# Changing the order in which the first two weight tiles of a projection meet the split activations, and the order inside a head norm, an attention and a scan

## The reference

```python
# one head of layer 0: o is normed per head (subln), then all heads meet wo
o = jnp.einsum('bhqk,bkhe->bqhe', a, v)
o = rmsnorm(o, subln) * (1.0 - lam_init)
y = o.reshape(...) @ wo
x = x + g1 * y
# every projection in front of an attention or feed-forward part reads a modulated norm
h = rmsnorm(x, norm_mix[i]) * (1.0 + sc1) + sh1
```

## Time and profile before

| what | value |
|---|---|
| median of 3 runs | 3529.85 us (3528.49 to 3533.06) |
| the profiled execution, its own time | 3529.11 us |
| its span (first to last instruction) | 3527.3 us |
| mean granted TensorE clock | 0.969 of 2.4 GHz |
| PE busy | 3268.6 us, 93% of the span |
| DVE, ACT, POOL busy | 2269.5, 1466.2, 332.9 us |
| head norm block, from the trace | about 444 to 477 us |
| neighbourhood attention | about 1324 to 1509 us |
| hgrn scan | about 2472 to 2611 us |

### The profile page before, as it was taken

One profiled execution on the slowest core, in us unless ns is written; L12 is line 12 of the kernel. 1 busy time (PEld: TensorE's weight loads), 2 busy tenths in 40 slices (PEclk: granted clock), 3 DMA queues, 4 the chain that ended last, 5 costly groups with the idle time before them and its releaser, 6 DMA issues. The chain is left out here.

```text
span 3527.3 us, 46837 instructions
## 1 busy us (share of the span) xinstructions
PE 3268.6 (93%) x18680; PEld 2681.7 (76%) x18680; DVE 2269.5 (64%) x2972; ACT 1466.2 (42%) x1948; POOL 332.9 (9%) x214
## 2 busy tenths in 40 slices
PE   7998989999998998889999998889889989999996
PEld 5887768888887896778787868779667766777774
DVE  6467756656656317758776555575665357888885
ACT  5216723212122116633233343433433246777774
POOL 0020000000000000000000004321100013222221
PEclk8999989999999999999999999999989999999998
DMA  6550013453542221045654229211013249999993
GB/s 238 192 172 13 1 48 93 134 167 119 168 127 87 66 75 55 22 126 184 212 176 148 55 76 273 57 37 49 25 42 90 72 185 363 383 374 369 378 364 109
DMA packets 371656, 522.46 MB, mean 148 GB/s; under 512 B 19618, under 2 KB 313122, under 8 KB 345872
## 3 DMA queue, kind: packets, MB, share of 16 engines
q1 hardware_dynamic: 362112, 503.25, 42.6%
q0 software_dynamic: 9360, 16.72, 1.4%
HBM read 484.46 MB, written 51.90 MB: 152 GB/s over the span
## 5 line engine op out<-in xcount | busy, mean ns | idle before, releaser
L270 DVE TENSOR_TENSOR lo<-exp_raw,exp_hi 128x2048 fp32r<-128x2048 f32 x192 | 438.9, 2290 | 65.3 <-ACT exp_hi L3548 65.3
L3548 ACT CAST exp_hi<-exp_raw 128x2048 fp32r<-128x2048 f32 x192 | 366.5, 1913 | 113.5 <-PE exp_down_acc L265 50.0
L263 PE MATMUL ffn_acc<-normed_hi,up_w_hi 128*128 128x512 f32 (+1 forms) x1056 | 377.1, 357 | 11.3 <-DVE lo L589 6.1
L264 PE MATMUL ffn_acc<-lo,up_w_hi 128*128 128x512 f32 (+1 forms) x1056 | 376.4, 356 | 0.0
L263 PEld LDWEIGHTS ffn_acc<-normed_hi,up_w_hi 128*128 128x128 f32 x1056 | 199.5, 189 | 44.2 <-DVE lo L270 7.0
L421 DVE SCALAR_TENSOR_TENSOR aside_w<-aside_w,aside_c 128x1024 f32<-128x1024 f32 x176 | 209.2, 1221 | 26.5 <-DMA aside_w<-in_ada_t 19.8
L264 PEld LDWEIGHTS ffn_acc<-lo,up_w_hi 128*128 128x128 f32 x1056 | 199.7, 189 | 31.1
L263 PE MATMUL ffn_acc<-gated_hi,down_w_hi 128*128 128x512 f32 (+1 forms) x528 | 190.9, 362 | 15.3 <-DVE lo L270 15.1
L1238 ACT ACTIVATE conv<-ffn_acc,vecs 128x768 f32<-128x768 f32 (+1 forms) x88 | 73.2, 882 | 290.2 <-PE ffn_acc L265 290.2
L264 PE MATMUL ffn_acc<-lo,down_w_hi 128*128 128x512 f32 (+1 forms) x528 | 189.9, 360 | 0.0
L265 PE MATMUL ffn_acc<-normed_hi,up_w_lo 128*128 128x512 f32 (+1 forms) x528 | 188.6, 357 | 0.0
(11 more groups left out here) (620 smaller groups left out, 8751.7 us busy)
## 6 DMA issues: line engine op xcount, KB each, us to landing
exp_raw<-in_w_experts SPq DMA_DIRECT2D x192, 1024.0 KB, 9.0
aside_w<-in_ada_t SPq DMA_DIRECT2D x176, 512.0 KB, 6.2
up_w<-in_ffn_up SPq DMA_DIRECT2D x88, 512.0 KB, 5.2
x_rows<-dn_zero SPq DMA_DIRECT2D x42, 384.0 KB, 5.4
y_rows<-dn_zero SPq DMA_DIRECT2D x42, 384.0 KB, 5.3
ada_w<-in_ada_first SPq DMA_DIRECT2D x8, 1024.0 KB, 12.3
v<-in_ada_t SPq DMA_DIRECT2D x16, 512.0 KB, 6.4
down_w<-in_ffn_down SPq DMA_DIRECT2D x16, 512.0 KB, 3.9
```

The costliest lines, as they stand in the source:

```text
L263: nc.tensor.matmul(out, left[0], right[0], start=start, stop=False)
L264: nc.tensor.matmul(out, left[0], right[1], start=False, stop=False)
L270: return engine.tensor_tensor(lo, value, hi.bitcast(F32), ALU.subtract)
L3548: nc.scalar.copy(hi[slot(e, j)][:], raw[tile(e, j)][:]).then_inc(tile_hi[j], 1)
```

## The change

Four orders are changed. No product is dropped.

1. In `Ring.multiply` and in the first visit of `ffn`, the products of a chunk with the activations' high part now come behind a wait for the high part alone, and only the product with the low part comes behind the wait for the low part.
2. `head_norm` is gone. A class `Heads` does its steps inside the residual of layer 0: squares and roots ahead of the residual's own work, then the scaling of chunk c + 2, the rounding and the low part of chunk c, and the products of chunk c interleaved. The rounding of this residual goes from DVE to ACT. Five matmuls on constants (`HEADS_IDLE`) stand between the sums and the spreading.
3. In `neighbourhood`, PE makes `scores` one step ahead instead of two, `values(g - 1)` before `turn(g, 0)`; ACT makes the exponentials of step g after the copies of step g - 1 instead of before them.
4. In `hgrn`, the low part of the next head's gates goes from DVE to POOL; the recurrence starts at level 1 and makes one step at each of the levels 4, 5 and 6. The semaphore of the states counts steps.

```diff
-    def multiply(self, pe, acc, chunks, ready, right, parts, between=None):
+    def multiply(self, pe, acc, chunks, high, ready, right, parts, between=None, first=None):
...
         for c in range(KD):
+            if first:
+                first(c)
+            pe.wait_ge(high, c + 1)
+            for u in range(2):
+                for a, b in parts:
+                    products_of_high(nc, acc[:, u, a:b], self.weights(u, c), right(c, a, b)[0], c == 0)
             pe.wait_ge(ready, c + 1)
             for u in range(2):
                 for a, b in parts:
-                    last = products(nc, acc[:, u, a:b], self.weights(u, c), right(c, a, b), c == 0, c == KD - 1)
+                    last = nc.tensor.matmul(acc[:, u, a:b], self.weights(u, c)[0], right(c, a, b)[1], start=False, stop=(c == KD - 1))
```

```diff
+class Heads:
...
+    def tensor(self, pe, parts):
+        nc, pick, ident = self.K.nc, self.K.const("pick"), self.K.const("ident")
+        for t in range(self.tok // P):
+            last = nc.tensor.transpose(self.spreads[0][0:KD, t * P:(t + 1) * P], self.sums[:, t, :], ident)
+        last.then_inc(self.floor_full, 1)
...
+        for _ in range(HEADS_IDLE):
+            nc.tensor.matmul(self.idle, ident, self.K.consts[:, 0:512], start=True, stop=True)
+        pe.wait_ge(self.split, 1)
+        for c in range(2):
+            self.spread(pe, c, parts)
+
+    def spread(self, pe, c, parts):
+        row = self.rows[:, c:c + 1].broadcast_to([KD, P])
+        if c >= 2:
+            pe.wait_ge(self.scaled, c - 1)
...
         def _(act):
+            if heads:
+                heads.squares(act)
             for n in range(2, 4):
                 ring.high(act, n)
+            if heads:
+                heads.roots(act)
+                for c in range(KD):
+                    heads.high(act, hi, c)
...
         def _(pe):
-            ring.multiply(pe, acc, KD, src_split, lambda c, a, b: (hi[:, c, a:b], lo[:, c, a:b]), parts)
+            if heads:
+                heads.tensor(pe, parts)
+            ring.multiply(pe, acc, KD, heads.rounded if heads else hi_ready, src_split, lambda c, a, b: (hi[:, c, a:b], lo[:, c, a:b]), parts,
+                          first=lambda c: heads and c + 2 < KD and heads.spread(pe, c + 2, parts))
```

```diff
                 if g >= 1:
                     turn(g - 1, 1)
                     turn(g - 1, 2)
-                if g + 2 < STEPS:
-                    scores(g + 2)
+                    if g + 1 < STEPS:
+                        scores(g + 1)
+                    values(g - 1)
                 if g < STEPS:
                     turn(g, 0)
-                if g >= 1:
-                    values(g - 1)
...
             for g in range(1, STEPS + 1):
-                if g < STEPS:
-                    exps(g)
                 if g >= 2:
                     take_values(g - 2)
                 take(g - 1)
+                if g < STEPS:
+                    exps(g)
```

```diff
+                if it + 1 < HEADS:
+                    raw, high, low = parts[it + 1]
+                    pool.wait_ge(gates_hi, it + 1)
+                    lo_of(nc.gpsimd, low, raw, high).then_inc(gates_lo, 1)
                 pool.wait_ge(e_out, it * 2 * PASSES + 2 * PASSES)
...
-                    if lev == 1 and it + 1 < HEADS:
-                        raw, high, low = parts[it + 1]
-                        dve.wait_ge(gates_hi, it + 1)
-                        lo_of(nc.vector, low, raw, high).then_inc(gates_lo, 1)
-                    if lev == EARLY:
+                    if lev == 1:
                         dve.wait_ge(ds_ready, it + 1)
...
-                        for st in range(1, NT - 1):
...
-                        dve.sem_inc(states, 1)
+                        step(1)
+                    if lev >= EARLY:
+                        step(lev - 2)
```

More of the change, by code:

```diff
@@ L265, in products, with products_of_high @@
     return nc.tensor.matmul(out, left[1], right[0], start=False, stop=stop)
+def products_of_high(nc, out, left, high, start):
+    nc.tensor.matmul(out, left[0], high, start=start, stop=False)
+    nc.tensor.matmul(out, left[1], high, start=False, stop=False)
 def lo_of(engine, lo, value, hi):
@@ L1031, in residual @@
+def residual(K, src, w, gate_at, tok, early, extra, following=None, sums=None):
     nc = K.nc
@@ L1069, in _ @@
         def _(dve):
+            if heads:
+                heads.vector(dve)
+                for c in range(2):
+                    heads.scale(dve, c)
             for c in range(KD):
[L1071 to L1072 removed]
+                if heads:
+                    dve.wait_ge(heads.rounded, c + 1)
+                else:
+                    nc.vector.tensor_copy(hi[:, c, :], src[:, c, 0:tok]).then_inc(hi_ready, 1)
+                    dve.wait_ge(hi_ready, c + 1)
                 lo_of(nc.vector, lo[:, c, 0:tok], src[:, c, 0:tok], hi[:, c, :]).then_inc(src_split, 1)
+                if heads and c + 2 < KD:
+                    heads.scale(dve, c + 2)
             for n in range(2, 4):
@@ L1196, in _ @@
             for c in range(KD):
+                pe.wait_ge(first.hi_ready, c + 1)
+                for s in range(2):
+                    for _, a, b in parts:
+                        products_of_high(nc, acc[:, 0, s, a:b], (wh[0][:, c, s, :], wl[0][:, c, s, :]), h[0][:, c, a:b], c == 0)
                 pe.wait_ge(first.ready, c + 1)
                 for s in range(2):
-                    last = up_chunk(0, s, c)
+                    for _, a, b in parts:
+                        last = nc.tensor.matmul(acc[:, 0, s, a:b], wh[0][:, c, s, :], h[1][:, c, a:b], start=False, stop=(c == KD - 1))
             last.then_inc(acc_full[0], 1)
```

157 lines of the change are left out of this document (68 added, 89 removed).

## The result

| | us |
|---|---|
| before, median of 6 runs beside it | 3533.64 (3528.49 to 3539.56) |
| changed, median of 6 runs | 3517.07 (3512.73 to 3522.25) |
| ratio | 0.9953 [0.9942, 0.9964] |
| the changed kernel once more, 6 runs | 3512.89, ratio 0.9940 [0.9926, 0.9955] |

The change makes the kernel faster, by 0.47% in the first comparison and 0.60% in the second: 17 and 21 us, 19 us taken together. The forecast was 31 us and 3498 us, with a range up to 3513. The direction was right, the size was not. Of the 19 us between the forecast 3498 and the measured 3517, 4.5 come from the base: the forecast subtracts from 3529.1, and the kernel before had a median of 3533.64 in the six runs beside the changed one. The other 14.5 are gain that did not come. The profiled execution took 3518.20 us, its span is 3516.4.

The account below looks back on a forecast made before the run. PE, busy 93% of the span, was taken as the bound. From 3529.1 us, 5.9 (projection starts), 6 (head norm), 10 (attention) and 9.3 (scan) were subtracted: 3498 us, own range 3490 to 3506, wider range 3488 to 3513.

Parts of the forecast that it names:

- The shift stays: Starts of projections: PE is slower than or equal to DVE after the earlier start, so 0.8 or 1.2 us a site is kept.
- the clock stayed up behind the shorter idle time: Starts of projections: a residual whose idle time shrinks may keep its clock; no size given.
- their second wait: Feed-forward second visits: PE's wait for their own weights' low part grows from 1.52 to 2.7 us.
- A wait of 0.3 replaces that of 0.56: period 5.15 us.: Attention: PE's wait for turn 0's copy replaces that for the values' copy; 28 steady steps at -0.30 give -8.4 us.
- the sign of being wrong: Attention: the prediction counts as wrong if a step is not shorter than 5.3 us.
- The head of the loop: Attention: one scores no longer stands ahead of the first values, -1.9 us.
- The rival on the other side: Attention: the chain of scores, maxima, exponentials and turns is met once per step; 8.9 us steps, +107 us, total 3615; chance 3%.
- By heads: -3, -2.4, -2.4, -1.5: Hgrn scan: gains in us of its four heads, sum -9.3, range -13 to -3.
- I price the low part's share of that at +1.35: Hgrn scan, start of a head: DVE's first products stand while POOL has the low part, costing 1.35 us.
- Level 1's load, priced at +0.15: Hgrn scan, level 1: copies, clears and step 1 (1.35 us) replace the low part (1.22 us), costing 0.15 us.
- I leave the clock out here: Hgrn scan: no clock effect priced, as 8 products after the idle time took 1.14 us, against 1.12 at full clock.
- about -15: Hgrn scan: what this part would come to without the low part on POOL, each head gaining 1.35 us more.

## Why the prediction was right or wrong

**First edit: right in size, for another reason.** I forecast 5.9, as time by which products start earlier. Measured are 8 in the total and 6.7 by stages, but part of that is luck. "The shift stays" failed at several starts: at layer 1's queries 0.8 us became 0.4 to 0.5, since the clock rises no earlier than before and the time won is spent at 1.2 GHz. The rest came from starts at which the clock stayed up behind the shorter idle time, named in the forecast but priced at 0 in the sum. The feed-forward visits gave nothing, as forecast; their second wait grew less than forecast (1.79 instead of 2.7 us in the first part). The block behind the hgrn features was missed: its start belongs to DVE's weights, and the products that end earlier only lengthen PE's idle time.

**Head norm: right.** Six us forecast, 5.6 to 5.9 in the stage. The first products started at 466.3, ahead of the forecast by the 1.6 us that all before them was early. Two errors beneath that partly cancel. A chunk took 3.16 us instead of 2.6 at the upper clock: its own twelve products 2.1 instead of 1.9, the four 8-row products 0.9 instead of 0.7, and 0.2 at the change between them. And the clock came back at 470.6 instead of 475.

**Attention: the step that failed.** "A wait of 0.3 replaces that of 0.56: period 5.15 us." The new wait is there with its size: without it a step takes 5.04, with it 5.36. What was wrong is that it replaces the old one whole. The forecast set 0.5 us of transposes into a gap of 0.56 and put the rest at nothing; measured, turn 1 still follows the values' copy, and about 0.12 us of that wait stay: the turns take 1.66 instead of 1.54 us. The weights' product, now behind the scores, takes 0.42 instead of 0.31, of which the values give back 0.07; why is open. So the 4.85 us that 5.15 needs beneath the new wait are 5.04. The sum itself had slipped as well: 5.45 - 0.56 + 0.3 is 5.19. A step is 0.09 instead of 0.30 us shorter, 2.5 instead of 8.4 us in all, and 5.36 is over the 5.3 that I had named as the sign of being wrong. The head of the loop gave 1.8 to 2.1, forecast 1.9, and one step beside POOL's low parts for the residual lost 1.0 (7.09 instead of 6.07 us, on PE a new wait for DVE's weights). 10 forecast, 2.6 to 2.9 measured. The rival on the other side, lookahead of one step, didn't come: the step fell to 5.04 as soon as the copy was short.

**Scan: mechanism right, sizes too large.** "By heads: -3, -2.4, -2.4, -1.5" were -2.1, -2.0, about 0 to -2, -0.9. Three terms were off. "I price the low part's share of that at +1.35" measured 2.98 - 0.82 = 2.16, with POOL's instruction itself at 3.10 instead of 2.43 us, as it began beside a product of DVE. Level 1's load, priced at +0.15, made a wait of 1.39 us at level 2 (0.94 in the variant without POOL's low part). And "I leave the clock out here": the scan before spent 20.5 to 23.9 us at 1.2 GHz, the changed one 17.1. 9.3 forecast; 4.7 by stages, 7 by the total.

Together 20 us by stages instead of 31: 7.2 are missing in the attention and 4.6 in the scan. The rule of the Trainium skill ("SBUF — State Buffer", section "SBUF: two separate sides") on the shared ports spoke in the right direction, and the trace has it with a larger number than I gave it. The "about -15" without it was too much: three heads have a low part on POOL, which makes -13.

## What to carry to other kernels

Price a reordering by what it leaves of the old wait and by PE's work in its new neighbourhood, not by the new wait alone. Take the time from the start of the last matmul before a wait to the start of the first behind it: if that is the same in both kernels, the old wait still holds, whatever the list of waits says. A pair of half-height matmuls that is parted cost more here than the wait that the parting was to fill. Where two engines hold each other up, ask which of them starts first, and let the one stand that nobody waits for. Where an engine idles a few us and then runs at half clock, look first for how to keep the idle time short; at the residual of layer 1 it was worth more than the shift itself (1.6 and 0.7 us). And when profiles of one program differ by 3 to 5 us, time a change of 0.1% by its stage in several profiles, and by the period of a loop, before its total.

## What the runs showed of the hardware

- Two 64-row matmuls on different rows of the array run side by side: four scores in 1.49 us together, 2.98 when the two of one head stand alone.
- DVE and POOL with SBUF operands hold each other up, and the order of their starts decided here who stood: DVE's product of 512 elements took 2.98 instead of 0.82 us behind POOL's subtraction, which itself took 3.10 instead of 2.43, having started 0.8 us before the end of another product of DVE. At level 4 it was DVE with 2.91 instead of 0.76 us, or, where DVE came first, POOL with 4.39 instead of 3.19.
- The granted clock fell behind 2.27 us of PE idle in six profiles of six and behind 1.54 us in none of ten (residual of layer 1), but behind 1.59 us in six of ten (gate features). Ahead of the head norm's spreading it was still 1.00 at the end of 4.0 us of idle and fell 1.1 to 1.3 us into the work in all but one of the profiles with five matmuls on constants; behind 0.6 us it stayed in two kernels and fell in a third. So the length of the idle time alone doesn't tell whether the clock falls.
